# Down-projection weight sums formed during the up projection and kept in DRAM, and 11 instead of 8 of 22 pairs by seven products

## The reference

```python
h = rms_norm(x, ln1); p = h @ w_in                     # retention and window attention from p
x = x + mix @ w_out
h = rms_norm(x, ln2)
a, b = jnp.split(h @ w_ffn_in, 2, axis=-1)             # up projection, 2 x 5632 columns
a = causal_depthwise_conv(a, conv_w, conv_b)
x = x + (jax.nn.gelu(a, approximate=False) * b) @ w_ffn_out   # down projection, 5632 x 2048
y = rms_norm(x, ln_f)
```

## Time and profile before

| | |
|---|---|
| median of 3 runs | 1096.52 us (1096.26 to 1096.79) |
| span of the profiled execution, first to last instruction | 1094.6 us |
| TensorE / VectorE / ScalarE / GpSimd busy | 1082.7 / 779.0 / 584.8 / 73.5 us |
| granted TensorE clock, mean | 0.998 |
| HBM read, written | 204.14 MB, 2.10 MB |

### The profile page before, as it was taken

One profiled execution on the slowest core, in us unless ns is written; L12 is line 12 of the kernel. 1 busy time (PEld: TensorE's weight loads), 2 busy tenths in 40 slices (PEclk: granted clock), 3 DMA queues, 4 the chain that ended last, 5 costly groups with the idle time before them and its releaser, 6 DMA issues.

```text
span 1094.6 us, 16578 instructions
## 1 busy us (share of the span) xinstructions
PE 1082.7 (99%) x5801; PEld 924.1 (84%) x5801; DVE 779.0 (71%) x1074; ACT 584.8 (53%) x790; POOL 73.5 (7%) x85
## 2 busy tenths in 40 slices
PE   8999999999999999999999999999999999999996
PEld 7888888888888888888888888888888888888885
DVE  6765776666655665665666657566568999989997
ACT  6445555555555454544545545445455666665663
POOL 2000111111000010101101001011010100000000
PEclk9999999999999999999999999999999999999999
DMA  9766555555566666666666666666666565755741
GB/s 340 265 195 191 161 166 153 168 167 166 167 184 187 173 183 194 186 189 189 191 191 185 186 188 190 191 190 185 185 189 190 172 201 187 248 183 181 260 163 77
DMA packets 146455, 206.84 MB, mean 189 GB/s; under 512 B 7555, under 2 KB 76001, under 8 KB 146160
## 3 DMA queue, kind: packets, MB, share of 16 engines
q1 hardware_dynamic: 145552, 204.17, 61.4%
q0 software_dynamic: 544, 1.69, 0.4%
q10 hardware_dynamic: 320, 0.47, 0.1%
HBM read 204.14 MB, written 2.10 MB: 188 GB/s over the span
## 4 chain that ended last, share of the span: by engine, by line
PE 98%; DVE 1%; DMA 0%; issue 0%; ACT 0%; DVEq 0%; ACTq 0%
PE acc L577 16%; PE acc L485 12%; PE acc L487 12%; PE acc L486 12%; PE acc L585 8%; PE bank_s L577 8%; PE bank_tr L577 8%; PE bank_tr L585 4%; PE bank_s L585 4%; PE bank_s L485 2%; PE bank_s L487 2%; PE bank_s L486 2%; PE bank_tr L485 2%; PE bank_tr L487 2%; PE bank_tr L486 2%; PE bank_s L633 0%
## 5 line engine op out<-in xcount | busy, mean ns | idle before, releaser
L1133 DVE TENSOR_TENSOR w_lo<-raw,w_hi 128x1024 fp32r<-128x1024 f32 x292 | 357.7, 1226 | 263.8 <-ACT w_hi L847 261.1
L847 ACT ACTIVATE w_hi<-raw 128x1024 fp32r<-128x1024 f32 x292 | 309.5, 1060 | 406.0 <-PE acc L487 137.2
L577 PE MATMUL acc<-h_both,w_hi 128*128 128x512 f32 x768 | 238.5, 392 | 0.0
L577 PEld LDWEIGHTS acc<-h_both,w_hi 128*128 128x128 f32 x768 | 137.9, 189 | 23.2 <-DVE rstd_row L1496 0.2
L585 PE MATMUL acc<-h_both,w_lo 128*128 128x256 f32 x768 | 154.2, 282 | 0.0
L585 PEld LDWEIGHTS acc<-h_both,w_lo 128*128 128x128 f32 x768 | 125.9, 191 | 7.5
L577 PE MATMUL bank_s<-h_both,w_hi 128*128 128x512 f32 x384 | 118.6, 390 | 0.0
L577 PE MATMUL bank_tr<-h_both,w_hi 128*128 128x512 f32 x384 | 118.6, 390 | 0.0
L485 PE MATMUL acc<-w_hi,h_both 128*128 128x512 f32 (+1 forms) x288 | 111.9, 389 | 1.0 <-DVE h_both L1147 1.0
L487 PE MATMUL acc<-w_hi,h_both 128*128 128x512 f32 (+1 forms) x288 | 109.0, 378 | 0.0
L486 PE MATMUL acc<-w_lo,h_both 128*128 128x512 f32 (+1 forms) x288 | 108.8, 378 | 0.0
(11 more groups left out here) (267 smaller groups left out, 1646.3 us busy)
## 6 DMA issues: line engine op xcount, KB each, us to landing
raw<-in_w_ffn_in SPq DMA_DIRECT2D x176, 512.0 KB, 3.6
raw<-in_w_ffn_out SPq DMA_DIRECT2D x88, 512.0 KB, 4.6
raw<-in_w_in SPq DMA_DIRECT2D x130, 256.0 KB, 3.0
raw<-in_w_out SPq DMA_DIRECT2D x32, 512.0 KB, 3.8
raw<-in_w_in SPq DMA_DIRECT2D x19, 512.0 KB, 10.2
x_res<-in_x SPq DMA_DIRECT2D x3, 512.0 KB, 8.6
decay<-table_decay POOLq DMA_DIRECT2D x1, 1024.0 KB, 9.1
lnf_row<-in_ln_f SPq DMA_DIRECT2D x1, 1024.0 KB, 7.5
```

What stands on the lines that cost most here:

```text
L577: ins = mm(banks[ft // 2][:, ft % 2, :], w_hi[:, slot, q * COLS + ft * P:q * COLS + (ft + 1) * P], h_both[:, 2 * k + q, :, :].rearrange("p ...
L847: run(w_hi[:, n % SPLIT, :], raw[:, n % RAW, :], ACT.Copy).then_inc(hi_ready, 1)
L1133: tt(w_lo[:, n % SPLIT, :], raw[:, n % RAW, :], w_hi[:, n % SPLIT, :].bitcast(F32), ALU.subtract).then_inc(lo_ready, 1)
```

## The change

In each of the first nine up groups that the loops hold, SP loads one pair's four weight blocks for each sweep into a new tile `stage`, VectorE forms the four sums there in tiles 12 to 15 (`stage_sums`), and SP stores the sums to a tensor `kept_sums` in DRAM. In the down projection SP then loads, for the nine staged pairs (3, 5 .. 19), the blocks that are still used and the stored sums straight into the raw ring, where such a pair takes four of the eight slots. Pairs 6 and 12 (`OWN`) become seven-product pairs too and form their sums in the down projection as before, also in the ring. High and low parts of the sums get a second buffer. SP's up loop begins one group later than before, and `others_out` of the first sweep moves from step 20 to 21. The scratch of software DMAs is halved.

```diff
-S_PAIRS = list(range(3, 18, 2))
+STAGED = list(range(3, 20, 2))
+OWN = [6, 12]
+S_PAIRS = sorted(STAGED + OWN)
-X_OUT_AT = (20, 43)
+X_OUT_AT = (21, 43)
...
+def raw_use(pair):
+    return 2 * (pair + sevens_before(pair))
...
+            def load_pair(r):
+                sweep, p = divmod(r, DOWN_PAIRS)
+                use, first = raw_use(r), PAIR_SLOT[r]
+                c0 = 2 * sweep * COLS
+                staged = is_seven(r) and not is_own(r)
+                for half in range(2):
+                    slot = first + half
+                    raw_free(use + half)
+                    if staged and half == 0:
+                        kept = kept_sums[sweep * STAGES + STAGED.index(p)]
+                        sp.dma_start(raw[:, slot, 0:COLS], w_ffn_out_v[:, 2 * p, c0:c0 + COLS]
+                                     ).then_inc(raw_landed[slot], 16)
+                        sp.dma_start(raw[:, slot, COLS:2 * COLS], kept[:, 0:COLS]).then_inc(raw_landed[slot], 16)
+                    else:
+                        sp.dma_start(raw[:, slot, :], w_ffn_out_v[:, 2 * p + half, c0:c0 + 2 * COLS]
+                                     ).then_inc(raw_landed[slot], 16)
+                if staged:
+                    slot = sum_slot(r)
+                    raw_free(use + 2)
+                    raw_free(use + 3)
+                    sp.dma_start(sum_raw(r), kept[:, COLS:4 * COLS].rearrange("p (a n) -> p a n", a=3)
+                                 ).then_inc(raw_landed[slot], 16)
...
+            def up_loads(f, k):
+                n = FFN_TILE + 2 * GROUP_TILES + k
+                load_up(f * GROUP_TILES + n, n % RAW, k % 8, f * COLS + (2 * COLS + k // 8 * D_FF))
+                if k in (11, 13):
+                    stage_store(f, (k - 11) // 2)
...
+            with sp.Fori(0, STAGES - 1) as f:
+                for k in range(GROUP_TILES):
+                    up_loads(f, k)
+                for j in range(2):
+                    sp.wait_ge(stage_stored[j], f * 16 + 16)
+                    stage_load(f + 1, j)
...
-            for m in range(16, 2 * FFT):
-                load_down_static(m)
+            for r in range(LAST_PAIR + 1):
+                load_pair(r)
...
+            def stage_sums(f, j, part):
+                b11, b12, b21, b22, fresh = (stage[:, j, i, :] for i in range(5))
+                if part == 0:
+                    dve.wait_ge(stage_landed[j], f * 16 + 16)
+                    tt(fresh, b22, b12, ALU.subtract).then_inc(stage_summed[j], 1)
+                    tt(b12, b12, b11, ALU.subtract).then_inc(stage_summed[j], 1)
+                else:
+                    dve.wait_ge(stage_summed[j], f * 4 + 2)
+                    tt(b22, b22, b12, ALU.subtract).then_inc(stage_summed[j], 1)
+                    dve.wait_ge(stage_summed[j], f * 4 + 3)
+                    tt(b21, b21, b22, ALU.subtract).then_inc(stage_summed[j], 1)
...
+                    if not last and k >= 12:
+                        stage_sums(turn, (k - 12) // 2, k % 2)
...
-                if r < LAST_PAIR and is_seven(r + 1):
+                if r < LAST_PAIR and is_own(r + 1):
                     weight_sums(r + 1)
```

More of the change, by code:

```diff
@@ L76 @@
 LAST_PAIR = 2 * DOWN_PAIRS - 1
[L80 to L82 removed]
+STAGED = list(range(3, 20, 2))
+OWN = [6, 12]
+S_PAIRS = sorted(STAGED + OWN)
+S_SLOT = {pair: i for i, pair in enumerate(STAGED + OWN)}
+S_SUMS = 8
+STAGES = len(STAGED)
 X_ADDS = 6
[L84 removed]
+X_OUT_AT = (21, 43)
 GAIN_AT = 18
@@ L114, in sevens_before, with is_own, own_before @@
     return sum(is_seven(p) for p in range(pair))
+def is_own(pair):
+    return pair % DOWN_PAIRS in OWN
+def own_before(pair):
+    return sum(is_own(p) for p in range(pair))
+def raw_use(pair):
+    return 2 * (pair + sevens_before(pair))
 def is_head_tile(n):
@@ L123, in landed_value, with down_raw_plan, sum_slot @@
     return 16 * sum(2 if is_head_tile(m) else 1 for m in range(n % RAW, n + 1, RAW))
+def down_raw_plan():
+    slots_of, landed, owner, count = {}, {}, {}, {}
+    for slot in range(RAW):
+        count[slot] = landed_value(DOWN_TILE - RAW + (slot - DOWN_TILE) % RAW)
+    for pair in range(2 * DOWN_PAIRS):
+        use = raw_use(pair)
+        first = (DOWN_TILE + use) % RAW
+        slots_of[pair] = first
+        staged = is_seven(pair) and not is_own(pair)
+        count[first] += 32 if staged else 16
+        count[first + 1] += 16
+        landed[pair] = [count[first], count[first + 1], 0]
+        owner[use] = owner[use + 1] = ("blocks", pair)
+        if is_seven(pair):
+            sums = (first + 2) % RAW
+            owner[use + 2] = owner[use + 3] = ("sums", pair)
+            if staged:
+                count[sums] += 16
+                landed[pair][2] = count[sums]
+    return slots_of, landed, owner
+PAIR_SLOT, PAIR_LANDED, RAW_OWNER = down_raw_plan()
+def sum_slot(pair):
+    return (PAIR_SLOT[pair] + 2) % RAW
 def build(nc, x, ln1, w_in, b_swa, ret_gn, sinks, w_out, ln2, w_ffn_in, conv_w, conv_b, w_ffn_out,
-          ln_f, ident_in, rope_in, mask_in, decay_in, y):
+          ln_f, ident_in, rope_in, mask_in, decay_in, y, kept_sums):
     x_v = x.rearrange("b (t p) d -> (b p) t d", p=P)
@@ L365, in build @@
         t_sum_ready = sem("t_sum_ready")
+        stage_landed = [sem(f"stage_landed{j}") for j in range(2)]
+        stage_summed = [sem(f"stage_summed{j}") for j in range(2)]
+        stage_stored = [sem(f"stage_stored{j}") for j in range(2)]
         t_hi_ready = sem("t_hi_ready")
@@ L413, in load_up, with raw_free @@
                 load(n, slot, w_ffn_in_v[:, 2 * k:2 * k + 2, bass.ds(first_col, COLS)])
[L415 to L422, removed]
+            def raw_free(use):
+                before = use - RAW
+                if before < 0:
+                    sp.wait_ge(lo_ready, DOWN_TILE + before + 1)
+                    return
+                what, pair = RAW_OWNER[before]
+                if what == "blocks":
+                    sp.wait_ge(lo_ready, DOWN_TILE + 2 * pair + 2)
+                    if is_own(pair):
+                        sp.wait_ge(t_sum_ready, 4 * own_before(pair + 1))
+                else:
+                    sp.wait_ge(t_lo_ready, sevens_before(pair) + 1)
@@ L1031, in g_round @@
                     act.wait_ge(tile_used, DOWN_TILE + 2 * (r - PAIR_RING + 1))
+                if r == 0:
+                    for j in range(2):
+                        act.wait_ge(stage_stored[j], 16 * STAGES)
                 if is_seven(r):
@@ L1453, in token_sums @@
             def token_sums(k):
-                first, last = S_PAIRS[0], S_PAIRS[-1]
-                step = S_PAIRS[1] - first
-                at = slice(2 * first, 2 * last + 1, 2 * step), slice(2 * first + 1, 2 * last + 2, 2 * step)
+                step, set_ = divmod(k, 2)
+                pairs = (STAGED, OWN)[set_]
+                gap = 2 * (pairs[1] - pairs[0])
+                at = slice(2 * pairs[0], 2 * pairs[-1] + 1, gap), slice(2 * pairs[0] + 1, 2 * pairs[-1] + 2, gap)
+                slots = slice(S_SLOT[pairs[0]], S_SLOT[pairs[-1]] + 1)
                 g11, g21 = g_tok[:, at[0], 0:P], g_tok[:, at[0], P:SEQ]
                 g12, g22 = g_tok[:, at[1], 0:P], g_tok[:, at[1], P:SEQ]
-                s2, s3, s4 = (g_sums[:, :, i, :] for i in range(3))
+                s2, s3, s4 = (g_sums[:, slots, i, :] for i in range(3))
                 if k == 0:
                     dve.wait_ge(g_ready, 2 * (GROUPS - 1))
+                    for j in range(2):
+                        dve.wait_ge(stage_stored[j], 16 * STAGES)
                 else:
```

120 lines of the change are left out of this document (74 added, 46 removed).

## The result

| | before | changed |
|---|---|---|
| median of 5 runs, us | 1096.26 (1095.85 to 1096.79) | 1101.70 (1101.09 to 1104.25) |
| ratio, 95% interval | | 1.0055 (1.0044 to 1.0066) |
| span of the profiled execution, us | 1094.6 | 1101.4 (its own time 1103.18) |

The change made the kernel slower by half a percent, where 0.35% faster was forecast. The page of the changed kernel: busy time, chain and HBM traffic.

What follows compares the result with a forecast made beforehand. The prediction took TensorE, busy 99% of the span, to bound the kernel. Its terms, -4.08 - 1.49 + 1.32 + 0.4 = -3.85 us, took 1096.52 to 1092.67, given as 1092.6 us, range 1091.0 to 1096.8.

Steps and rivals of the forecast that it cites:

- Three products less: Down projection: pairs 6, 12 and 19 of each sweep go from 24 matmuls to 21 on TensorE, -4.08 us.
- The first sweep's waits go: Down projection: with 12 of 16 weight-sum formations gone, VectorE runs ahead and TensorE's first-sweep waits go, -1.49 us.
- The tail: End of the kernel: the cross sums' additions can't start before pair 41 is done, +1.32 us.
- Up projection and stores: Up projection: VectorE's eight additions and SP's four 1 MB transfers more per group cost 0 us.
- The raw ring: Down projection, runs of three seven-product pairs: nothing stalls while landings keep their median; +0.4 us, ends 0 and 5.8.
- the prediction's own sign of being wrong: TensorE's steps in the up projection open, or landings in the runs pass 5.5 us as a rule.
- d: Lateness in us of all landings in the down projection's runs; a sweep loses (3d - 2.3) + d once that is positive.
- the ring runs short: Rival, pairs 11 to 14 of each sweep: late landings cost 2 x (4d - 2.3) us; chance 0.10 light, 0.08 heavy.
- the second rival: Rival, down projection's loads: the queue streams at 340 GB/s, not 392; 1.0 to 3.4 us lost, chance 0.08.

Runs made afterwards that it cites:

- e1: Changed kernel without own sums: pairs 6 and 12 of each sweep back to eight products, nine staged sevens; 1095.04 us (ratio 0.9989).
- e3: Changed kernel with the sums of pairs 6 and 12 not formed, whatever stands in their slots used instead; 1092.39 us (ratio 0.9966).
- e5: Changed kernel with ten instead of eight ring slots in the down projection, activations' sums of only seven pairs formed; 1092.12 us (ratio 0.9960).
- e7: As e1, but the nine staged sevens at pairs 2, 4, ..., 18 instead of 3, 5, ..., 19; 1093.91 us (ratio 0.9976).
- e9: Changed kernel with staged pairs fetching down-weight rows of the same bytes and shapes in place of their kept sums; 1101.18 us (ratio 1.0044).
- e2: Changed kernel with VectorE forming the sums of pairs 6 and 12 behind, not ahead of, the preceding pair's low parts; 1093.03 us (ratio 0.9971).
- e6: Changed kernel with the blocks of pairs 6 and 12 issued ahead of the kept sums of pairs 5 and 11; 1100.36 us (ratio 1.0038).

## Why the prediction was wrong, step by step

- *Three products less, -4.08:* right. 5801 - 5783 = 18 matmuls, and two sevens take 9.52 us.
- *The first sweep's waits go, -1.49:* right wherever the ring does not stall: in e1, e3 and e5 TensorE has no wait from pair 0 to pair 42, with VectorE at 63.97 to 74.32 us of 80; e5 still forms the own sums. For e1 the sum of this step, of 6 matmuls x 0.2267 and of the tail gave 1094.7; it measured 1095.04.
- *The tail, +1.32:* right; 1.1 to 1.4 by e7 against e1. In the changed kernel the addition starts 0.90 us behind pair 42's first matmul, where 0.83 was forecast:

```profile
1081.22 0.69 DVE L1702 TENSOR_TENSOR u_sum<-u_sum,bank_s 128x512 f32<-128x512 f32 x1 [0.55 <-ACT u_sum L1226]
```

- *Up projection and stores, 0:* right, by the window of 447 to 491.5 (34.5 of the 33 to 36 us forecast for VectorE) and the traffic of 237 and 21 MB.
- *The raw ring, +0.4:* **this step failed.** By the medians it is 1101.70 less 1092.1 to 1092.4 (e5 and e3, whose rings or sums don't bind), 9.3 to 9.6 us, and by the ratios 9.8 to 10.4; the profiled execution, 1.5 us above the median, shows 11.0. Without this term the forecast was 1092.27, and e5 and e3 lie within 0.15 us of it. That they lie so near is in part luck: both leave some other work out, and their chips differ by 0.36 us in the kernel before.

The step took "as long as landings keep their median nothing stalls" with a pair landing 5.1 us after its first issue, from stretches of the kernel before in which a pair was two transfers and little stood ahead of it; the 4.3 there is the median of one pair's two loads. In the changed kernel the 512 KB loads took 6.6 us in the median, which is the prediction's own sign of being wrong (past 5.5 us as a rule). Windows of the changed kernel, columns as in the earlier trace rows: from pair 6's first issue to its landing, in two parts; from pair 12's first issue nearly to its landing; and two stretches behind the first stall:

```profile
869.36:875.00 5.64, 5.64 (x26) 4.67 (x25) 3.94 (x4) 2.75 (x3) 0.00 (x0) 1.00 0.86 303
875.00:877.60 2.60, 2.60 (x13) 2.17 (x12) 0.00 (x0) 2.07 (x4) 0.00 (x0) 1.00 0.10 38
904.43:911.00 6.57, 6.57 (x31) 5.44 (x30) 3.93 (x4) 6.55 (x7) 0.00 (x0) 1.00 0.90 356
...
885.00:888.00 3.00, 3.00 (x15) 2.25 (x13) 3.00 (x3) 0.00 (x0) 0.00 (x0) 1.00 0.92 193
889.00:895.00 6.00, 3.72 (x17) 2.74 (x15) 3.60 (x5) 4.17 (x4) 0.00 (x0) 1.00 1.02 414
```

Pair 12 landed 7 us after its first issue. In that time 2.34 MB moved: 1.05 of its own behind 1.29 of the pairs ahead. At the 392 GB/s that the prediction went by, instead of 356, they would have been in 0.6 us sooner (an estimate), which leaves 1.3 of this pair's 1.9 us of lateness. So for this pair the term that was missing is the bytes that stand ahead, and the rate is the smaller part. Pair 6 landed 8.2 us after its first issue, with 1.81 MB moved, 0.76 ahead of its own. Here the queue was slower, 303 GB/s to 875.0, and the last 0.1 MB took 2.6 us, at a busy share of 0.10. In e9 that slow end is missing (4 GB/s from 875 to 876, then nothing); VectorE waited 1.67 us for pair 6 there instead of 3.16, and TensorE 1.27 for pair 7 instead of 2.41. What makes such an end is not known.

The loss asks for d = 1.75 in the prediction's formula, near the heavy form of "the ring runs short" (d = 1.6: 1100.5, chance 0.08). The landings were not that even: pair 6 was 3.1 us late, pair 7 about 2.5, pair 12 1.9, and the runs at 5 to 7 lost as well as those at 11 to 13. "Late ones came singly" was read from a kernel whose queue was half empty (0.57); here one late landing made the next issue late.

Whether 392 GB/s was wrong too, the second rival, these runs do not settle, since the full queue has no one rate: 193 and 414 GB/s in the two stretches above, with 326 to 328 as means of windows that hold both kinds. The kernel before shows the same spread, 301 GB/s from 3 to 10 us at a share of 0.97 and 392 from 10 to 20 at 1.06. What sets the slow stretches was not tested; pair 12, 1.3 us late even at 392, shows that the step fails without them.

The mechanism that the prediction did count, VectorE's forming in front of a low part, was taken as 2.66 us of work. What it cost was the wait in front of that work, and e2 shows that it need not stand there.

Open: why the run at pairs 27 to 29 had no wait in the changed kernel's profiled execution, while the later run of that sweep had one of 2.64 us. VectorE stood only 0.47 us in front of the sums of pair 28, against 3.16, 1.65 and 2.14 in the other runs; why those blocks came in time is not known. In the later run, and in none of the others, SP issues the 1 MB gain vector, at 1037.54, right behind the blocks of pair 36 (1036.68), which ScalarE could round only from 1045.18. It may have slowed them. No run was made for either.

## What to carry to other kernels

A landing time read from a half-empty queue (4.3 us a load, at a DMA share of 0.57) was no price for one in a full queue (6.6 us; 0.94 and 0.99 in windows of the runs): work the lateness out from the bytes that will stand ahead, at a rate taken from a stretch where the queue is as full and as mixed, and leave room: here that rate ran from 193 to 414 GB/s. Where an engine waits for a transfer in its order of instructions, as VectorE did for 3.16 us, ask what stands behind it and which load the things behind it release; to put the work on the newest load behind work whose data were there gave 8.7 us here (e2). A ring two pairs deep turned one late landing into a late issue, and so into another late landing; one slot pair more ended that (e5: 1092.12 us, and no wait from pair 0 to pair 42).

## What the runs showed of the hardware

The DMA queue moved 326 to 328 GB/s over 10 to 12 us of the runs at a busy share of 0.94 to 0.99, and 392 over 10 us near the start of the kernel before. Within the runs it moved 193 GB/s at 0.92 and 414 at 1.02: the busy share does not give the rate.

In e6 TensorE's matmuls stood 0.43 us apart behind a wait of 2.74 us, twice the usual distance, and the granted clock of the 3.5 us behind that wait was 0.59 in the mean: 0.50 from 1046.00 to 1048.70. TensorE of e6, the first rows behind the wait and the seventh:

```profile
1046.03 0.77 PE L609 MATMUL acc<-w_hi,g_hi 128*128 128x512 f32 x1 [2.74 <-DVE w_lo L1687]
1046.59 0.63 PE L610 MATMUL acc<-w_lo,g_hi 128*128 128x512 f32 x1
1047.02 0.63 PE L611 MATMUL acc<-w_hi,g_lo 128*128 128x512 f32 x1
...
1048.73 0.47 PE L609 MATMUL acc<-w_hi,g_hi 128*128 128x512 f32 x1
```

Windows of e6, behind the wait and after it:

```profile
1046.00:1049.50 3.50, 3.47 (x9) 2.79 (x10) 1.88 (x3) 2.94 (x2) 0.00 (x0) 0.59 0.98 386
1049.50:1053.00 3.50, 3.50 (x17) 2.88 (x16) 3.50 (x3) 2.79 (x3) 0.00 (x0) 1.00 0.94 323
```

From the first to the seventh it is 2.70 us, where six matmuls usually take 1.36: 1.3 us on top of the wait. In the changed kernel the waits of 2.41 and 2.64 us brought no such rows: the granted clock was 1.00 in the 2.87 us behind each.
